# A hybrid decoder step on one core: who reads the unmasked logits, how three key blocks are summed, and the query copies

## The reference, cut to what matters

```python
def stick_breaking(q, k, v, bias, q_offset):
    """A[t,s] = sigmoid(z_ts) * prod_{s<j<t} (1 - sigmoid(z_tj)), s < t strictly; log space."""
    z = jnp.einsum('bqhd,bkhd->bhqk', q.astype(f32), k.astype(f32)) * (HD_B ** -0.5)
    z = z + bias.astype(f32)[None, :, None, None]
    mask = jnp.arange(Lk)[None, :] < (q_offset + jnp.arange(Lq))[:, None]
    u = jnp.where(mask, jax.nn.log_sigmoid(-z), 0.0)
    rev_excl = lax.cumsum(u, axis=3, reverse=True) - u
    A = jnp.where(mask, jnp.exp(jax.nn.log_sigmoid(z) + rev_excl), 0.0)
    return jnp.einsum('bhqk,bkhd->bqhd', A, v.astype(f32))
```

## Time and profile before

| | |
|---|---|
| median of 3 runs | 1500.66 us (1500.21 to 1502.5) |
| the profiled execution | 1502.18 us |
| its span, first to last instruction | 1500.4 us |
| TensorE busy | 1476.8 us |
| VectorE busy | 1181.6 us |
| ScalarE busy | 827.7 us |
| GpSimd busy | 333.6 us |
| mean granted TensorE clock | 0.999 |

### The profile page before, as it was taken

How to read it: one execution, slowest core, us unless ns; L and a number is a source line. 1 busy time by engine, 2 the same in 40 slices (tenths; PEclk the granted TensorE clock), 3 DMA queues, 4 the chain that set the end, 5 groups by cost and what they waited for, 6 DMA issues and landing times.

```text
span 1500.4 us, 33609 instructions
## 1 busy us (share of the span) xinstructions
PE 1476.8 (98%) x12928; PEld 1397.7 (93%) x12928; DVE 1181.6 (79%) x2014; ACT 827.7 (55%) x1312; POOL 333.6 (22%) x330
## 2 busy tenths in 40 slices
PE   8999999999999999999999999999999999999998
PEld 8999999989999999999998888887699999999998
DVE  7866666667898988989834888888789989898753
ACT  6554444435664645546533777777756546364543
POOL 3000000002332232232142122112233332232221
PEclk9999999999999999999999999999999999999999
DMA  6233333223777877777425555543338777778621
GB/s 191 58 87 88 87 87 87 87 87 87 139 170 157 179 164 161 176 153 155 135 85 176 186 191 197 184 156 114 100 86 168 177 159 168 166 157 187 142 85 64
DMA packets 237716, 205.83 MB, mean 137 GB/s; under 512 B 8268, under 2 KB 224404, under 8 KB 237588
## 3 DMA queue, kind: packets, MB, share of 16 engines
q1 hardware_dynamic: 151346, 147.34, 31.6%
q0 software_dynamic: 68160, 47.20, 20.4%
q10 hardware_dynamic: 18082, 9.48, 2.3%
HBM read 192.19 MB, written 11.80 MB: 136 GB/s over the span
## 4 chain that ended last, share of the span: by engine, by line
PE 94%; DVE 2%; ACT 2%; issue 1%; DMA 0%; DVEq 0%; ACTq 0%
PE acc L2904 23%; PE acc L3227 18%; PE pL L3227 12%; PE pM L3227 9%; PE acc L3327 6%; PE pO L3227 3%; PE acc L3165 2%; PE pL L3025 1%; PE pL L3368 1%; PE pO L3401 1%; PE pM L3382 1%; PE acc L3444 1%; PE acc L3461 1%; PE pM L3094 1%; PE pM L3388 1%
## 5 line engine op out<-in xcount | busy, mean ns | idle before, releaser
L658 POOL TENSOR_TENSOR wlo<-wraw,whi 128x512 fp32r<-128x512 f32 x40 | 56.2, 1435 | 449.3 <-ACT whi L795 449.3
L2904 PE MATMUL acc<-xa_hi,whi 128*128 128x288 f32 x544 | 125.0, 311 | 0.2 <-DVE hT L2355 0.2
L881 ACT ACTIVATE hi<-wraw 128x1024 fp32r<-128x1024 f32 x60 | 63.7, 1061 | 104.2 <-DVE wraw L2025 104.2
L864 ACT ACTIVATE hi<-wraw 128x1024 fp32r<-128x1024 f32 x60 | 63.7, 1061 | 103.0 <-PE acc L3227 102.8
L2904 PE MATMUL acc<-xa_hi,wlo 128*128 128x288 f32 x544 | 116.5, 296 | 0.0
L2904 PE MATMUL acc<-xa_lo,whi 128*128 128x288 f32 x544 | 116.1, 295 | 0.0
L3227 PE MATMUL acc<-X_lo,hi 128*128 128x288 f32 x384 | 113.3, 295 | 0.0
L3227 PE MATMUL acc<-X_hi,lo 128*128 128x288 f32 x384 | 113.3, 295 | 0.0
L3227 PE MATMUL acc<-X_hi,hi 128*128 128x288 f32 x384 | 113.1, 294 | 0.0
L2040 DVE TENSOR_TENSOR lo<-wraw,hi 128x1024 fp32r<-128x1024 f32 x60 | 73.3, 1222 | 42.4 <-ACT hi L864 42.4
L3227 PE MATMUL acc<-H_hi,hi 128*128 128x288 f32 x336 | 99.3, 296 | 1.3 <-DVE lo L2046 1.3
(11 more groups left out here) (549 smaller groups left out, 5135.2 us busy)
## 6 DMA issues: line engine op xcount, KB each, us to landing
wraw<-in_w_up_dram SPq DMA_DIRECT2D x64, 512.0 KB, 6.4
wraw<-in_w_down_dram SPq DMA_DIRECT2D x64, 512.0 KB, 5.5
Kp<-in_cache_k_dram SPq DMA_DIRECT2D x32, 512.0 KB, 4.4
Vp<-in_cache_v_dram SPq DMA_DIRECT2D x32, 512.0 KB, 5.4
wraw<-in_w_in_a_dram SPq DMA_DIRECT2D x30, 512.0 KB, 5.6
wraw<-in_w_up_dram POOLq DMA_DIRECT2D x32, 256.0 KB, 4.8
S_even<-in_w_up_dram POOLq DMA_DIRECT2D x32, 256.0 KB, 6.3
...
```

Of the source, the lines that this page charges most:

```text
L658: ins = pool.tensor_tensor(wlo[s][:, k:k + 2, :], wraw[s][:, k:k + 2, :], whi[s][:, k:k + 2, :].bitcast(F32), ALU.subtract)
L864: act.activation(blocks4(hi02), by_rows(G % 2)[:, 0], ACT.Copy).then_inc(piece_hi, 1)
L881: act.activation(blocks4(hi31), by_depth(G % 2)[:, 0], ACT.Copy).then_inc(piece_hi, 1)
L2904: last = pe.matmul(acc[a][:, hf, 0:HALF], w[s][:, k, a * P:(a + 1) * P], x[k][:, hf * HALF:(hf + 1) * HALF], start=(k == 0 and n == 0), st ...
```

## The change

1. In turns 0 to 6 the unmasked columns of each unit are read from the bank by ScalarE: an `Identity` activation with the scale and a per-partition bias (`bias_two`, a two-column tile that GpSimd copies out of `bias_h`), ahead of the three of `softplus`, which wait for it. VectorE's instruction for them is left out there. `logits(j, g)` for g = 1, 2 waits for ScalarE's reading too.
2. In turns 0 to 6 GpSimd adds block 1 and the sum of 2 and 3 (`later_sum_0`), ScalarE and VectorE split it (`later_high_0`, `later_low_0`, 256 columns each), and the `ones_r` products over `LATER[1]` for g = 2 are left out. The last turn is as before.
3. The four copies of `queries` become two of twice the size.

```diff
+        S1_COLS, S0_COLS, N_U = slice(256, 384), slice(512, 768), 10
+        H_AT, S1_HI, S0_HI = [(1, 2, 3, 4, 7, 9), (1, 2, 3, 4, 7, 8)], (5, 6), (8, 10)
+        U_AT = [(1, 2, 4, 5, 7, 9), (1, 2, 4, 5, 7, 8)]
+        LATER_AT = [(1, 2, 4, 6, 8, 10), (1, 2, 4, 6, 7, 8)]
...
+        def last_turn(j):
+            return isinstance(j, int) and j == NPAIR - 1
+
+        def soft_count(j, n, k):
+
+            return 24 * j + (3 * n if last_turn(j) else 4 * n + 1) + k
...
+                wait(pool, soft, 24 * j)
+                pool.tensor_copy(bias_two[:], bias_h[:, bass.ds(2 * j, 2)])
...
+            def later_sum_0(j, hh):
+
+                pool.wait_ge(u_lo, N_U * j + hh + 4)
+                pool.wait_ge(bias_ready, 5 * j + 2 + hh)
+                pool.tensor_tensor(tl[2 + hh][:, P:3 * P], tl[2 + hh][:, P:3 * P], tl[hh][:, P:3 * P], ALU.add
+                                   ).then_inc(bias_ready, 1)
...
                 masked_bias(j + 1)
+                later_sum_0(j, 0)
+                later_sum_0(j, 1)
...
             def softplus(j, n):
                 g, hh = divmod(n, 2)
                 act.wait_ge(B_free[hh], 4 * j + 2 + g)
-                soft3(Am[hh][:, GCOL[g]:GCOL[g] + GW[g]], tl[n][:, 0:GW[g]], 18 * j + 3 * n, soft)
+                if not last_turn(j):
+                    c1, c2 = GCOL[g] + len(GROUPS[g]) * P, GCOL[g] + GW[g]
+                    act.activation(Am[hh][:, c1:c2], pL[:, hh, len(GROUPS[g]) * P:GW[g]], ACT.Identity, scale=SCALE,
+                                   bias=bias_two[:, hh:hh + 1]).then_inc(soft, 1)
+                    act.wait_ge(soft, soft_count(j, n, 0))
+                soft3(Am[hh][:, GCOL[g]:GCOL[g] + GW[g]], tl[n][:, 0:GW[g]], soft_count(j, n, 0), soft)
...
+            def later_high_0(j, hh):
+
+                act.wait_ge(bias_ready, 5 * j + 5 + hh)
+                act.wait_ge(R_full, 7 * j + hh + 4)
+                act.activation(uh[hh][:, S0_COLS], tl[2 + hh][:, P:3 * P], ACT.Copy).then_inc(u_hi, 1)
...
                 u_high(j, 4)
+                later_high_0(j, 0)
                 weights(j, 0)
                 weights(j, 1)
                 weights(j, 2)
                 u_high(j, 5)
+                later_high_0(j, 1)
...
-                dve.tensor_scalar(Am[hh][:, c1:c2], pL[:, hh, nd * P:GW[g]], SCALE, bias_h[:, bass.ds(2 * j + hh, 1)],
-                                  ALU.mult, ALU.add).then_inc(B_free[hh], 1)
+                if last_turn(j):
+                    ins = dve.tensor_scalar(Am[hh][:, c1:c2], pL[:, hh, nd * P:GW[g]], SCALE,
+                                            bias_h[:, 2 * j + hh:2 * j + hh + 1], ALU.mult, ALU.add)
+                ins.then_inc(B_free[hh], 1)
...
                 minus_later(j, 3)
+                later_low_0(j, 0)
                 past_later(j + 1)
                 u_low(j, 5)
+                later_low_0(j, 1)
...
                     pe.wait_ge(B_free[hh], 4 * j + 1 + g)
+                if g and not last_turn(j):
+                    pe.wait_ge(soft, soft_count(j, 2 * g - 1, 0))
...
-                later = [(LATER[g], GW[g])] if g < 2 else [(LATER[2], GW[2]), (LATER[1], GW[2])]
+                later = [(LATER[2], GW[2]), (LATER[1], GW[2])] if g == 2 and last_turn(j) else [(LATER[g], GW[g])]
```

More of the change, by code:

```diff
@@ L182, in yoco_step @@
         attn_o = qT
-        (kf, vf, khi, klo, qhi, qlo, kr, vr, uh0, ul0, ul1, Am0, tl0, tl1, tl2, tl3, tl4, bias_neg) = arena(
+        (kf, vf, khi, klo, qhi, qlo, kr, vr, uh0, ul0, ul1, Am0, tl0, tl1, tl2, tl3, tl4, bias_neg, bias_two) = arena(
             ar, [("kf", [P, T], F32), ("vf", [P, T], F32), ("khi", [P, SEQ], F32R), ("klo", [P, SEQ], F32R),
@@ L187, in yoco_step @@
                  ("tl0", [P, 384], F32), ("tl1", [P, 384], F32), ("tl2", [P, 384], F32), ("tl3", [P, 384], F32),
-                 ("tl4", [P, 512], F32), ("bias_neg", [P, 2, P], F32)])
+                 ("tl4", [P, 512], F32), ("bias_neg", [P, 2, P], F32), ("bias_two", [P, 2], F32)])
         (uh1, Am1, KT, zbS, tlS, RS, pastO, newE, newO, QB, Oc, kvn, zbN, tlN, qnew, tl5) = arena(
@@ L752, in later_sum_1 @@
             def later_sum_1(j, hh):
-                pool.wait_ge(u_lo, N_U * j + U_AT[hh])
+                pool.wait_ge(u_lo, N_U * j + hh + 1)
                 pool.tensor_tensor(tl[hh][:, S1_COLS], tl[hh][:, S1_COLS], tl[hh][:, 0:P], ALU.add).then_inc(bias_ready, 1)
+            def later_sum_0(j, hh):
[3 more added lines that the diff above has]
+                                   ).then_inc(bias_ready, 1)
             def turn_sums(j):
@@ L2506, in queries @@
                         QB[rows].rearrange("p (i e) c -> p i (e c)", e=2).rearrange(
[L2507 to L2512, removed]
-                        qT[rows, :, bass.ds(SEQ + NEW * s, NEW)].rearrange("p (i e) n -> p i e n", e=2)[:, :, 1, :]
+                            "p i (g h n) -> p i g h n", h=2, n=NEW)[:, :, 0:4:3, hh, :],
+                        qT[rows, :, bass.ds(SEQ + NEW * s, NEW)].rearrange("p (i e) n -> p i e n", e=2)
                         ).then_inc(QB_ready, 1)
@@ L2585, in logits_in @@
                 if g == 0:
-                    dve.wait_ge(bias_ready, 1 if isinstance(j, int) and j == 0 else 3 * j - -1)
+                    dve.wait_ge(bias_ready, 1 if isinstance(j, int) and j == 0 else 5 * j - 1)
                 nd = len(GROUPS[g])
                 c0, c1, c2 = GCOL[g], GCOL[g] + nd * P, GCOL[g] + GW[g]
-                dve.scalar_tensor_tensor(out=Am[hh][:, c0:c1].rearrange("p (b t) -> p b t", t=P),
+                ins = dve.scalar_tensor_tensor(out=Am[hh][:, c0:c1].rearrange("p (b t) -> p b t", t=P),
                                          in0=pL[:, hh, 0:nd * P].rearrange("p (b t) -> p b t", t=P), scalar=SCALE,
                                          in1=bias_neg[:, hh:hh + 1, :].to_broadcast([P, nd, P]), op0=ALU.mult, op1=ALU.add)
-                dve.tensor_scalar(Am[hh][:, c1:c2], pL[:, hh, nd * P:GW[g]], SCALE, bias_h[:, bass.ds(2 * j + hh, 1)],
-                                  ALU.mult, ALU.add).then_inc(B_free[hh], 1)
+                if last_turn(j):
+                    ins = dve.tensor_scalar(Am[hh][:, c1:c2], pL[:, hh, nd * P:GW[g]], SCALE,
+                                            bias_h[:, 2 * j + hh:2 * j + hh + 1], ALU.mult, ALU.add)
+                ins.then_inc(B_free[hh], 1)
             def sp_add(j, n):
@@ L2597, in sp_add @@
                 tv = tl[n][:, 0:GW[g]]
-                dve.wait_ge(soft, 18 * j + 3 * n + 3)
+                dve.wait_ge(soft, soft_count(j, n, 3))
                 dve.wait_ge(B_free[hh], 4 * j + 2 + g)
@@ L2605, in u_low @@
                 cols = slice(GCOL[g], GCOL[g] + GW[g])
-                dve.wait_ge(u_hi, N_U * j + H_AT[n])
+                dve.wait_ge(u_hi, N_U * j + H_AT[last_turn(j)][n])
                 dve.wait_ge(sp_done, 6 * j + n + 1)
@@ L2614, in later_low_1, with later_low_0 @@
                 dve.tensor_tensor(ul[hh][:, S1_COLS], tl[hh][:, S1_COLS], uh[hh][:, S1_COLS].bitcast(F32), ALU.subtract
+                                  ).then_inc(u_lo, 1)
+            def later_low_0(j, hh):
+                dve.wait_ge(u_hi, N_U * j + S0_HI[hh])
+                dve.tensor_tensor(ul[hh][:, S0_COLS], tl[2 + hh][:, P:3 * P], uh[hh][:, S0_COLS].bitcast(F32), ALU.subtract
                                   ).then_inc(u_lo, 1)
@@ L3378, in later_sums @@
                     pe.wait_ge(n_dve, 6 * j + 1)
-                pe.wait_ge(u_lo, N_U * j + U_AT[n])
+                pe.wait_ge(u_lo, N_U * j + U_AT[last_turn(j)][n])
                 tri = slice(GCOL[g], GCOL[g] + GW[g])
@@ L3439, in past_logits @@
                 pe.wait_ge(Td_free, 4 * s + 2 * h2 + 2)
-                pe.wait_ge(QB_ready, 4 * s + 4)
+                pe.wait_ge(QB_ready, 2 * s + 2)
                 wait(pe, n_dve, 6 * s)
```

8 lines of the change are left out of this document (2 added, 6 removed).

## The result

The changed kernel takes 1521.99 us (median of 4 runs, 1521.34 to 1522.72), the kernel before 1501.11 us over the runs beside it: 20.9 us more, a ratio of 1.0140 with a 95% interval of 1.0128 to 1.0152. I had forecast 1514.2 and a range of 1507 to 1520. The direction was right and so was the first mechanism; the size was too small by a third, and the time lies outside the range.

What follows compares the result with a forecast made beforehand. The prediction took TensorE's work plus its waits as the bound, with ScalarE's queue to `t_copy(j+1, 6)` as the turn's chain. Seven turns at 1.93 us, 13.5 us, on 1500.66 gave 1514.2, range 1507 to 1520.

Steps and rivals of the forecast that it cites:

- What bounds the kernel: Each turn, ScalarE's queue up to `t_copy(j+1, 6)` is the chain; TensorE waits 0.3 us for it before `past_logits`.
- What the change adds to the chain: Five `Identity` activations ahead of `t_copy(j+1, 6)` lengthen ScalarE's queue by 2.39 us a turn.
- What it gives back there: Ahead of `t_copy(j+1, 6)`, ScalarE starts 0.26 us earlier and three short waits, 0.45, vanish; the copy comes 1.70 later.
- From there to the turn's end: Behind `t_copy(j+1, 6)`: `past_soft` 2.0 us late, `past_sp` 1.75, `past_weights` 2.1, `past_transposed` 1.9.
- The edits that cost nothing: GpSimd's new work, `later_high_0` and fewer query copies add nothing; GpSimd's sum is ready 1.0 us ahead of ScalarE.
- Those steps last 1.58 whatever `later_sums(j, 5)` costs: From `past_transposed` to `past_values`: 1.58 us as before, since `past_values` needs the transposed weights copied out by VectorE.
- The four removed products: In TensorE's `later_sums(j, 4)` and `(j, 5)`: 0.48 us a turn saved, 3.4 in seven turns, but counted as nothing.
- Rival B: More waits: `Identity` nearer 0.7 us at 384 columns, or `later_high_0` standing for GpSimd; 17.9 us slower, 1518.6; 11%.
- A: The chain behind the copy absorbs its extra and removed products count: 1.46 us a turn, 10.2 in seven, 1510.9; 13%.
- C: ScalarE's run hides 2.4 us or more of waits for VectorE, where `Identity` fits: 3.4 us faster, 1497.3; 8%.
- D: TensorE's clock falls to 1.2 GHz for a tenth of each turn: 23 us slower, 1537; 2%.
- E: The change does not do what it says, or two of its parts cancel: 1500.7; 4%.

Runs made afterwards that it cites:

- e1: The kernel before with only part 1 of the change (ScalarE reads the unmasked columns): 1514.42 us, ratio 1.0083.
- e5: The changed kernel with ScalarE's `t_copy(j+1, 6)` moved between unit 4's `Identity` and its three activations: 1520.77 us.
- e4: The changed kernel with GpSimd's `later_sum_0` over 2 columns in place of 256, all waits and other instructions kept: 1515.95 us.
- e7: The kernel before with only part 2 of the change, and VectorE's `later_low_0(j, 1)` moved behind `minus_later(j, 4)`: 1505.79 us.
- part 2 alone: The kernel before with only part 2 of the change (the block sums and their 256-column split): 1507.12 us, ratio 1.0041.
- e6: The kernel before with only part 2 of the change, and GpSimd's `later_sum_0` over 2 columns in place of 256: 1503.68 us.

## Why the prediction was right and wrong

- **What bounds the kernel** held in the main: ScalarE's queue is the turn's chain, and lengthening it cost 13.1 us (e1). Its end is not `t_copy(j+1, 6)`, as I had it, but `past_soft` (e5).
- **What the change adds to the chain** held. The estimates were 362, 471 and 580 ns; the activations took 347, 471 and 570:

```profile
L1446 ACT ACTIVATE Am<-pL,bias_two 128x384 f32<-128x384 f32 x8 | 4.6, 570 | 0.0
L1446 ACT ACTIVATE Am<-pL,bias_two 128x256 f32<-128x256 f32 x8 | 3.8, 471 | 0.1
...
L1446 ACT ACTIVATE Am<-pL,bias_two 128x128 f32<-128x128 f32 x8 | 2.8, 347 | 0.0
```

- By the figure of the Trainium skill (ScalarE: Activation LUTs, What ACT_TABLE_LOAD costs) the estimates were 387, 493 and 600, which is 22 to 40 ns above these rows; the rows of the same kernel were the better source.
- **What it gives back there** held: unit 0 starts 0.24 us earlier (893.12, against 889.53 before, each from its `KT` copy), and the three short waits went (0.48, 0.95 and 0.41 us from start to start, where they were 0.64, 1.10 and 0.55). One piece was wrong: the release of `past_logits` before was VectorE's copy 7, not ScalarE's copy 6, which hid 0.2 us. Further on this did not count, since `past_soft` came 2.08 late all the same.
- **From there to the turn's end**: `past_soft` and `past_sp` held within 0.1 us. The step that failed first came then: "Ahead of the scan stands one new instruction, `later_low_0(j, 0)`". It does, at its 0.33 us, but two old instructions ahead of the scan became 0.31 and 0.54 us longer, 0.85 a turn for which the sum had no term.
- **The edits that cost nothing** is where this was lost: I asked of GpSimd's sums only whether they would be ready in time (margin 1.0 us), not what they do to VectorE while they run. e4 puts this at 6.0 us of the 20.9. The margin itself went too: the sums took 1.18 to 1.23 us each beside VectorE, not 0.61, and `later_high_0(j, 0)` started at 913.75, 0.67 behind `u_high(j, 4)` at 913.08, which takes about 0.52 of the queue: GpSimd was about 0.15 late, where I had it 1.0 early.
- "Those steps last 1.58 whatever `later_sums(j, 5)` costs" failed: they last 1.96. I followed what `past_values` waits for, and not that `later_sums(j, 5)` waits for `minus_later(j, 4)`, which now queued behind two splits. e7 puts this at 1.3 us in the time, 2.0 by its turn.
- A small miss the other way: the transposes took up 0.34 us of the lateness (3.03 to 2.69 in the table), not 0.2, since the crossing from ScalarE that I had at 0.25 takes 0.06. Together, per turn: 0.09 up to `past_sp`, 0.84 to `past_weights`, -0.14 and 0.38 behind it make 1.17 us over the forecast's 1.9 at `past_values`.
- The four removed products gained nothing that a run shows, as forecast. TensorE's busy time did not fall by their 3.4 us either (1477.5 against 1476.8); ends of products are modelled, and why it did not is open.
- Rival B (more waits, 1518.6) named the right side, but for other reasons (a dearer `Identity`, a late sum). Rivals A, C, D and E did not come about; the granted clock stayed at 1.00 in the loop, with waits of up to 1.5 us in it.

The account, from the runs: 13.1 us for ScalarE's queue (e1), 3.4 for GpSimd's hold on VectorE in part 2 alone (e6), the remaining 2.4 of part 2 for the two splits in VectorE's queue (what e6 still costs): 18.9. The whole change costs 2.0 more, which the intervals alone can't tell from nothing; the traces have a reason for it. Where ScalarE is late, GpSimd's sums lie beside longer instructions, and the hold is 0.85 us a turn against 0.55 in part 2 alone (6.0 us in e4 against 3.4 in e6).
